# Attention steps of a hybrid decoder layer, reordered: heads first, begun inside the fourth query projection

## What is computed

```python
x = x + 0.5 * SwiGLU_1(rms(x))
u, q, k, v = split(rms(x) @ w_in)         # 512 | 512 | 128 | 128 columns
q, k = rope(rms_head(q)), rope(rms_head(k))
pool = (window_mean_w(u) - u) @ pool_w    # w = 2, 4, 8, 16 for the four groups of 128 channels
attn = softmax with a sink per head, window of 128 keys, 8 heads over 2 key heads
x = x + concat(pool * scale, attn) @ w_out
x = x + 0.5 * SwiGLU_2(rms(x))
```

## Time and profile before

| | us |
|---|---|
| median of 3 runs | 893.75 (893.37 to 893.81) |
| the profiled execution, its own time | 894.7 |
| its span in the trace | 892.6 |
| PE busy in the span | 881.3 |
| DVE busy | 658.9 |
| ACT busy | 393.5 |
| POOL busy | 32.4 |

### The profile page before, as it was taken

One profiled execution on the slowest core, in us unless ns is written; L12 is line 12 of the kernel. 1 busy time (PEld: TensorE's weight loads), 2 busy tenths in 40 slices (PEclk: granted clock), 3 DMA queues, 4 the chain that ended last, 5 costly groups with the idle time before them and its releaser, 6 DMA issues.

```text
span 892.6 us, 17094 instructions
## 1 busy us (share of the span) xinstructions
PE 881.3 (99%) x7118; PEld 864.1 (97%) x7118; DVE 658.9 (74%) x954; ACT 393.5 (44%) x631; POOL 32.4 (4%) x37
## 2 busy tenths in 40 slices
PE   9999999999999999999988999999999999999998
PEld 8999999999999999999867999999999999999998
DVE  7969556997479976743777588997469984699844
ACT  8635213554135544433465446554125552255520
POOL 0000000000000000013322000000000000000000
PEclk9999999999999999999997999999999999999999
DMA  7233313423333323423201313333424424244241
GB/s 270 92 124 126 131 48 122 144 89 95 130 119 119 119 84 121 155 80 106 95 1 62 110 68 118 126 112 102 147 72 154 131 74 153 79 146 130 81 122 60
DMA packets 42892, 98.57 MB, mean 110 GB/s; under 512 B 4128, under 2 KB 4768, under 8 KB 42816
## 3 DMA queue, kind: packets, MB, share of 16 engines
q1 hardware_dynamic: 40912, 94.67, 31.8%
q10 hardware_dynamic: 1904, 2.81, 0.9%
HBM read 93.53 MB, written 3.60 MB: 109 GB/s over the span
## 4 chain that ended last, share of the span: by engine, by line
PE 93%; DVE 4%; ACT 1%; issue 1%; POOLq 0%; POOL 0%; DVEq 0%
PE ps L565 43%; PE ps L693 15%; PE ps L695 15%; PE ps L694 15%; PE ps L596 1%; ACT prob L1315 1%; PE ps L587 1%; DVE small L1799 1%; DVE prob L1815 1%; PE ps L752 1%; PE ps L612 0%; PE ps L966 0%; PE ps L835 0%; DVE wlo L1431 0%; DVE hlo L1558 0%
## 5 line engine op out<-in xcount | busy, mean ns | idle before, releaser
L693 PE MATMUL ps<-xhi,whi 128*128 128x260 f32 (+1 forms) x1092 | 310.2, 284 | 0.1
L695 PE MATMUL ps<-xhi,wlo 128*128 128x260 f32 (+1 forms) x1092 | 310.1, 284 | 0.0
L694 PE MATMUL ps<-xlo,whi 128*128 128x260 f32 (+1 forms) x1092 | 309.7, 284 | 0.0
L693 PEld LDWEIGHTS ps<-xhi,whi 128*128 128x128 f32 x1092 | 205.4, 188 | 0.8 <-issue 0.6
L695 PEld LDWEIGHTS ps<-xhi,wlo 128*128 128x128 f32 x1092 | 205.5, 188 | 0.0
L694 PEld LDWEIGHTS ps<-xlo,whi 128*128 128x128 f32 x1092 | 205.5, 188 | 0.0
L1502 DVE TENSOR_TENSOR wlo<-full,whi 128x1024 fp32r<-128x1024 f32 (+1 forms) x117 | 160.3, 1394 | 0.0
L1049 ACT CAST whi<-raw 128x1024 fp32r<-128x1024 f32 (+1 forms) x76 | 76.3, 1004 | 180.6 <-PE ps L565 171.6
L565 PE MATMUL ps<-hhi,whi 128*128 128x268 f32 (+1 forms) x690 | 140.5, 285 | 0.3
L565 PE MATMUL ps<-hlo,whi 128*128 128x268 f32 (+1 forms) x690 | 140.2, 285 | 0.0
L565 PE MATMUL ps<-hhi,wlo 128*128 128x268 f32 (+1 forms) x690 | 139.8, 284 | 0.0
(11 more groups left out here) (191 smaller groups left out, 1084.8 us busy)
## 6 DMA issues: line engine op xcount, KB each, us to landing
full<-gu SPq DMA_DIRECT2D x78, 512.0 KB, 4.4
raw<-d SPq DMA_DIRECT2D x32, 448.0 KB, 3.4
full<-gu SPq DMA_DIRECT2D x39, 256.0 KB, 2.7
raw<-d SPq DMA_DIRECT2D x16, 512.0 KB, 3.4
raw<-gu SPq DMA_DIRECT2D x10, 512.0 KB, 3.8
raw<-w_in SPq DMA_DIRECT2D x10, 512.0 KB, 3.6
raw<-w_out SPq DMA_DIRECT2D x8, 512.0 KB, 4.5
xT<-x SPq DMA_DIRECT2D x8, 268.0 KB, 5.5
```

The source lines that it names most:

```text
L693: nc.tensor.matmul(dst, whi_t, xhi_t, start=(first and pr == 0), stop=False, skip_group_check=True)
L694: nc.tensor.matmul(dst, whi_t, xlo_t, start=False, stop=False, skip_group_check=True)
L695: last = nc.tensor.matmul(dst, wlo_t, xhi_t, start=False, stop=(pr == KC - 1), skip_group_check=True)
```

## The change

Steps are ordered by head pair first: step i handles block i % 4 and head pair i // 4. Steps 0 to 3 thus need only q0 and q1. The sums of squares, roots and reciprocals of the queries are taken in two halves (q0 and q1, then q2 and q3 with the decode queries). The steps' banks are nsum, turn and pair[1] in turn; all of u0 to u3 and the pool maps use pair[0]; the decode products use the second banks of turn and nsum. PE's, ACT's, DVE's and POOL's lists are written anew. The waits of POOL's window sums for given steps go (after_probs), and so does ACT's wait of the first out_probT for the decode exponential. The buffer prob moves to where upn, p1c, u2c, u4c and t4 lie. Counts of semaphores are adapted.

```diff
-    banks_of = [ps[:, 2:4, :], ps[:, 4:6, :], ps[:, 6:8, :]]
-    outpair = [ps[:, 0:2, :], ps[:, 6:8, :]]
+    banks_of = [nsum, turn, pair[1]]
+    outpair = pair
...
-        return k // 2, 2 * (i % 2) + k % 2
+        return k // 2, 2 * (i // QT) + k % 2
...  PE
-        project(4, half[0])
+        project(4, [0, 1])
         q_sums(0)
-        project(4, half[1])
+        project(4, [2, 3, 4])
+        q_sums(1)
+        project(4, [5, 6, 7])
         project(5, half[0])
-        q_sums(1)
-        project(5, half[1])
-        project(6, half[0])
-        q_sums(2)
-        project(6, half[1])
...
-        project(7, half[0])
-        q_sums(3)
-        project(7, half[1])
-        pool_map(0)
-        scores(0)
-        scores(1)
...
+        scores(0)
+        scores(1)
+        project(5, half[1])
+        project(6, half[0])
+
+        turn_probs(0)
+        scores(2)
+        attend(0)
+        q_sums(2)
+        q_sums(3)
+        project(6, half[1])
+
+        turn_probs(1)
+        scores(3)
+        attend(1)
+        decode_scores()
+        project(7, [0, 1, 2, 3, 4])
+        decode_turn()
+        project(7, [5, 6, 7])
+
+        turn_probs(2)
+        scores(4)
+        pool_map(0)
+        attend(2)
+        project(8, half[0])
+
+        turn_probs(3)
+        scores(5)
+        attend(3)
+        decode_turn_back()
+        project(8, half[1])
+
+        turn_probs(4)
+        scores(6)
+        pool_map(1)
+        attend(4)
+        decode_attend()
+        project(9, half[0])
+
+        turn_probs(5)
+        scores(7)
+        attend(5)
+        project(9, half[1])
+
+        turn_probs(6)
+        pool_map(2)
+        attend(6)
+        turn_probs(7)
+        out_product(1, [0, 1, 4, 5])
+        attend(7)
+        pool_map(3)
+        out_product(1, [2, 6, 7])
+        out_product(0, [0, 1, 4, 5, 2, 6, 7])
+        out_product(0, [3])
+        out_product(1, [3])
         for d in range(2, KD):
...  ACT, behind spread_z(2)
+        q_root(0).then_inc(root_ready, 1)
         split_next(4)
         spread_z(3)
-        split_next(5)
+        exps(0)
         spread_z(4)
+        out_probT(0)
+        exps(1)
+        out_hi(0)
+        q_root(1)
...
+        split_next(5)
+        out_probT(1)
+        exps(2)
+        out_hi(1)
+        split_next(6)
+        exps(3)
...
+        exps(7)
+
+        split_next(9)
+        out_probT(6)
+        pool_hi(2)
+        out_hi(6)
+        out_probT(7)
+        out_hi(7)
+        pool_hi(3)
...  DVE, behind rotate(1)
+        rotate(2)
+        dve.wait_ge(root_ready, 4)
+        half_q = QT * KVH * 2
+        nc.vector.reciprocal(qnrm[:, 1, 0:half_q], qnrm[:, 0, 0:half_q]).then_inc(inv_ready, 1)
         take_z(3)
         split_next(4)
-        rotate(2)
+        dve.wait_ge(inv_ready, 4)
+        maxima(0)
+        rotate(3)
+        maxima(1)
         take_z(4)
-        split_next(5)
-        rotate(3)
+        normalise(0)
+        rotate(4)
+
+        maxima(2)
+        normalise(1)
+        out_lo(0)
...
+        normalise(6)
+        maxima(7)
+        out_lo(5)
+
+        take_u(3)
+        split_next(9)
+        normalise(7)
+        pool_out(2)
+        out_lo(6)
+        out_lo(7)
+        pool_mean(3)
+        pool_out(3)
...  POOL
-        after_probs = {(2, 0): 2, (3, 0): 6, (3, 2): 7}
...
+        window_sums(0)
         window_sums(1)
-        pool.wait_ge(dprob_ready, 1)
         pool_lo(0)
         window_sums(2)
-        pool.wait_ge(prob_ready, 3)
         pool_lo(1)
-        window_sums(3, 0, 2)
-        pool_lo(2)
-        window_sums(3, 2)
         pool.wait_ge(dohi_ready, 1)
...
+        window_sums(3)
+        pool_lo(2)
         pool_lo(3)
```

More of the change, by code:

```diff
@@ L566, in product @@
                                                 start=(k == 0 and w is whi and not lo),
-                                                stop=(k == tiles - 1 and w is wlo))
-            if not ks or ks[-1] == tiles - 1:
+                                                stop=(k == end and w is wlo))
+            if not ks or ks[-1] == end:
                 last.then_inc(unit_done, 1)
@@ L938, in attend, with decode_scores @@
                         last.then_inc(attended, 1)
[L940 to L946, removed]
+        def decode_scores():
+            pe.wait_ge(newk_placed, 1)
+            pe.wait_ge(dq_ready, KVH)
+            pe.wait_ge(probT_ready, 2)
+            for b in range(NDEC):
+                last = nc.tensor.matmul(turn[:, 1, b * HEADS:(b + 1) * HEADS], ckT[:, b, :], dq[:, b, :, :],
@@ L973, in _ @@
-        pool_map(0)
-        scores(0)
-        scores(1)
[L976 to L981, removed]
+            last.then_inc(douts_filled, 1)
         def out_product(d, ks=None):
@@ L988, in out_product @@
                 elif d == 1:
-                    pe.wait_ge(olo_ready, 2 * QT - 2)
+                    pe.wait_ge(olo_ready, 6)
                 else:
                     pe.wait_ge(evacuated, E_OUT + d - 1)
[L993 to L1023, removed]
@@ L1364, in _ @@
         nc.scalar.activation(dsmall[:, 4:5], dsmall[:, 2:3], ACT.Exp).then_inc(dexp_ready, 1)
+        out_hi(2)
+        split_next(7)
+        exps(4)
+        out_probT(3)
         pool_hi(0)
[L1366 to L1384, removed]
+        out_hi(3)
+        exps(5)
+        out_probT(4)
+        split_next(8)
+        out_hi(4)
+        pool_hi(1)
+        exps(6)
+        out_probT(5)
+        act.wait_ge(douts_kept, 1)
+        nc.scalar.copy(mhi[:, NG:NG + GQ, SEQ:NOUT], dout[:, :, :].rearrange("p b j -> p j b")
+                       ).then_inc(dohi_ready, 1)
+        out_hi(5)
+        exps(7)
[6 more added lines that the diff above has]
+        pool_hi(3)
         for d in range(KD):
@@ L1888, in _ @@
         nc.vector.tensor_tensor(dsmall[:, 2:3], dsmall[:, 1:2], dsink, ALU.add).then_inc(dnmax_ready, 1)
-        pool_mean(1)
+        take_u(1)
+        normalise(3)
+        pool_out(0)
+        maxima(4)
+        out_lo(2)
         dve.wait_ge(dexp_ready, 1)
@@ new lines, in _ @@
+        pool_mean(1)
+        split_next(7)
+        normalise(4)
+        maxima(5)
+        out_lo(3)
+        dve.wait_ge(dprobs_filled, 1)
+        nc.vector.tensor_copy(dprobT[:, :], nsum[:, 1, 0:HD]).then_inc(dprobs_kept, 1)
+        take_u(2)
+        normalise(5)
+        pool_out(1)
+        maxima(6)
+        split_next(8)
+        out_lo(4)
+        dve.wait_ge(douts_filled, 1)
+        for g in range(KVH):
+            rows = slice(g * HD, (g + 1) * HD)
+            last = nc.vector.tensor_copy(dout[rows, :, :],
+                                         turn[rows, 1, 0:HD].rearrange("p (b h) -> p b h", b=NDEC)[
+                                             :, :, g * GQ:(g + 1) * GQ])
@@ L1930, in _ @@
+        last.then_inc(douts_kept, 1)
+        pool_mean(2)
+        normalise(6)
[9 more added lines that the diff above has]
+        pool_out(3)
         for d in range(KD):
```

187 lines of the change are left out of this document (77 added, 110 removed).

## The result

The change makes the kernel slower: 898.24 us median of 6 runs (896.42 to 899.89) against 893.78 (893.27 to 895.51), ratio 1.0043, 95% interval 1.003 to 1.0055. A second set of six runs of the same file gave 899.07 beside 893.89, ratio 1.0053 (1.0038 to 1.0068). The ratios and intervals go by all runs of both kernels, so they differ a little from the ratio of the medians: by the medians the loss is 4.5 and 5.2 us, by the ratios 3.8 and 4.7. The forecast was 889.2.

What follows compares the result with a forecast made beforehand. PE, busy 99% of the span, was taken as the bound. 403.5 + 86.8 of work + waits 0.6, 1.2, 2.4, 2.0, 1.95 = 498.5; the walk's 498.15 was taken, 4.5 us under 502.7: median 889.2, range 886.9 to 893.0.

Steps and rivals of the forecast that it cites:

- 4.9 for the clock: PE at 478.0 to 488.7 us: the old order's slow-clock stretch goes, 4.9 of at most 5.1 us taken off.
- I take 479.7: End of normalise(7) on DVE, held beside POOL's sums by 0.6 + 1.0 us; 478.1 if free of them.
- The walk of the lists: All engines' lists followed from scores(0) at 414.0 to output unit 2, which starts at 498.15 against 502.7 before.
- waits of 0.6 and 1.2: PE's two early waits for step probabilities, 0.6 us at about 423 and 1.2 at about 426.
- table loads and SP's late queue: ACT's extra table loads (2 x 1.28 us) and SP's output weights, delayed from 419.5 to 435.7, make PE wait for nothing.
- PE's own work: PE from 403.5 to output unit 2: no stage matmul added or removed, about three fewer switches; 86.8 us of work.
- 0.8 for small gaps in the output units: PE's small idle gaps in the output units, 0.8 us taken off the old trace's 99.2 us.
- free end at 478.1: normalise(7) on DVE ends at 478.1 if POOL's sums do not hold it; 1.6 us less, kept for the range.
- The waits of 2.0 and 1.95: PE waits 2.0 us at pool_map(3) behind pool_mean(3), and 1.95 at output unit 2 for its weight split.
- rival (a): Slow clock returns in the stretch from 474.2 to 480 or 424 to 430; price 3 to 5 us; chance 0.15.
- Rival (b): DVE between 428 and 484, held by 15 untied POOL instructions, becomes a slower bound; up to 896 us; chance 0.11.
- Rival (c): Steps do not begin early: late q1 rotation or half root delays scores(0), up to 3 us, 892; chance 0.07.

Runs made afterwards that it cites:

- a_warm_fit: Changed kernel with empty matmuls, three in front of turn_probs(7) and two in front of pool_map(3), sized to fit those waits; 894.98 us, ratio 1.0014 to the kernel before.
- a_sums_held: Changed kernel with one wait added: POOL's four sums of the last group start only when step 7's probabilities are normalised; 895.71 us, ratio 1.0008 to the kernel before.
- b_warm: Kernel before the change with two empty matmuls of 0.88 us each in its wait in front of attend(5); 892.33 us, ratio 0.9988 to the unedited kernel before.
- a_mean_first: Changed kernel with DVE's pool_mean(3) moved in front of out_lo(6) and out_lo(7); 894.32 us, ratio 1.0000 to the kernel before.
- a_unit0_first: Changed kernel with output unit 0 finished three blocks before output unit 1 instead of one; 896.37 us, ratio 1.0024 to the kernel before.
- b_sums_free: Kernel before the change with POOL's waits for given steps taken out; 897.06 us, ratio 1.0045 to the unedited kernel before.

## Why the prediction was wrong

The step that weighs most is the term "4.9 for the clock": it was booked as a gain, with full clock assumed for the new order, and the new order lost more to the clock than the old one. The second is the end of the lists, "I take 479.7", where the mechanism was right and the size was not. Both are measured at the start of output unit 2, counted from scores(0), as each trace begins a few tenths of a microsecond apart. The forecast had 498.15 - 414.0 = 84.15 us, the changed kernel took 506.61 - 413.82 = 92.8, and a_warm_fit, the same order at full clock, 502.03 - 414.29 = 87.7. So 3.6 of the 8.6 us are there without the clock, and 5.0 are the clock. In a_warm_fit:

```profile
414.29 0.60 PE L922 MATMUL ps<-maskb,identb 128*128 128x512 bf16 x2
...
475.68 1.04 PE L937 MATMUL ps<-fixed,prob 128*128 128x128 f32 x8
...
483.24 1.09 PE L937 MATMUL ps<-fixed,prob 128*128 128x128 f32 x8 [0.61 <-DVE prob L1863]
...
502.03 0.48 PE L571 MATMUL ps<-mhi,whi 128*128 128x260 f32 x2 [1.83 <-DVE wlo L1479]
```

By steps:

- **The walk of the lists** was right in its early half: scores(0) forecast at 414.0 and without a wait, found at 413.8; waits of 0.6 and 1.2 forecast, 0.1 to 0.5 (in four profiles) and 1.04 found; no wait from step 1 to 5, found; table loads and SP's late queue cost nothing, found. The three sets of transfers landed 1.7, 2.1 and 1.5 us behind the end of their issues (the rotations start at 410.56, 418.39 and 427.05), where I took 2.0: right within 0.6 us.
- **PE's own work** was sized 1.2 us short: at full clock turn_probs(6) comes 61.4 us behind scores(0), forecast 60.2. The two sets of sixteen decode products took 1.8 us each where four times the row of 0.34 gives 1.4; the rest is not placed. The sum also takes off 0.8 for small gaps in the output units and puts none back for the new order, which has the same units; the trace of before has only 99.2 - 92.7 - 6.4 = 0.1 us of idle time outside its waits there. The forecast followed the walk, which does not use that term.
- **"I take 479.7"** for normalise(7), the contention at the end, failed in size. turn_probs(7) came at 483.24 in a_warm_fit, 3.25 late counted from scores(0): 1.2 are PE's own work, 1.1 the hold, and 0.9 stand in front of the split, mostly a wait that the sum lacks. The hold: I gave each DVE instruction group one, 0.6 + 1.0 = 1.6. The split was not held at all, and normalise(7) was held three times, 1.03 - 0.16 + 2.93 - 1.14 = 2.7. The wait: the split stood 1.16 us idle for ACT's copy whi, which ACT makes behind exps(7) (the row at 479.87 above; the same 1.16 in a_warm_fit), and a free end at 478.1 leaves only about 0.4 for it. a_sums_held takes the whole hold away: the wait falls by 2.7 and the time by 3.1 us. The wait of 0.9 in front of attend(6), for a copy of ACT that stands behind the same whi, is not in the forecast either; it costs nothing, as turn_probs(7) behind it has 3.4 to wait anyway.
- **The waits of 2.0 and 1.95** at pool_map(3) and unit 2 were right in place and size: 2.3 and 1.8. The forecast waits sum to 8.15 us, against 6.4 in the old order, so on waits alone the change was forecast slower by 1.8. That sign was right in part by luck: at full clock the old order waits 8.0 us (b_warm: 6.1, and 1.9 that its empty matmuls fill), so 8.15 would have been a tie. The changed order waits 10.0 there (a_warm_fit, the filled time counted), 2.0 more.
- **"4.9 for the clock"** turned the forecast to a gain. It was credited in full to the change, as certain, with clock 1.00 assumed after it. Both halves failed. The fall cost the kernel before 3.0 to 3.2 us, not 4.9 (b_warm), as waits reappear when PE is faster. And the changed kernel, forecast with a wait of 2.4, one of 2.0 and one of 1.95 close to one another, fell three times. The rival (a) had this mechanism; it was given 0.15 and one fall, since a stretch with 3.6 us of waits had kept its clock.

Rival (b) named the right engines and the wrong place: in the middle steps the held instructions are covered, and its 15 full microseconds did not come (DVE's scalings are 4.9 us longer in all). Rival (c) did not occur.

At full clock the account closes: before 891.5 (b_warm, six runs), changed 893.7 (a_warm_fit, two runs), 2.3 slower, of which 2.0 are the waits. The clock adds 2.8 to the kernel before (894.3, the median of 72 runs) and 5.0 to the changed one (898.7), 2.2 more. Together 4.4 or 4.5.

## What to carry to other kernels

Do not book a low-clock stretch of the old trace as a gain: ask first what the waits alone give, and then whether the new order has fewer waits near dense work, since the clock followed them here and took the loss from 2.3 to 4.4 us. A reordering that fills the middle moves the waits to the ends, so look at what is left to lay over the last step before the first. And where waits of one engine look useless, find which other engine they keep it away from; price each meeting by how many of the other's instructions lie beside it and which of the two begins first.

## What the runs showed of the hardware

Behind a wait of 1.83 us between dense products stood a low stretch: granted clock 0.55 from 508.2 to 511.5, the fall 1.1 us behind the wait's end. In the kernel before the fall came 0.5 us behind a wait of 1.84 (478.45), but another wait of 1.89 had none. The same list of PE also falls in some profiles and not in others (near 429: yes in the changed kernel and a_mean_first, no in a_sums_held and a_unit0_first), and the mean clock of one kernel varies (0.990 to 0.996 in twelve runs of the changed one). The Trainium skill, TensorE: Matmul & The Clock Gate, Part 1, says that an idle TensorE is throttled and a busy one released. The runs agree in direction, and one fall came inside a wait (483.9); but those at 429.2, 478.45 and 507.8 came with the engine at work again, and in some runs only. That matmuls without a use raise the clock and shorten the time (mean clock 0.9973 against 0.9927, 3.5 us, in a_warm_fit) is shown here directly.

DVE's four scalings take 1.14 us alone, 2.17 beside one POOL instruction, 2.93 in the changed kernel, and 3.52 and 4.10 beside three in b_sums_free: about 0.8 to 1.0 us for each POOL instruction met, nearly POOL's own duration of 1.07. From its chain of waits:

```profile
446.15 3.52 DVE prob L1815 x4
...
479.46 4.10 DVE prob L1815 x4
```

Which of the two is held follows in these traces from which began first. The DVE splits and small two-input instructions that began while a sum ran were held (425.02, 1.87 us, behind a sum of 424.75; 481.01 above); a reciprocal, with one input, was not (445.94 in b_sums_free, 0.18 us inside a sum). A split that began first was not, and the sum was held instead: the split at 479.87 took its 1.23, and the sum at 479.94 took 2.08 where 1.07 is free; the split at 436.72 took 1.21, and the sum at 436.77 took 2.08.

```profile
436.72 1.21 DVE L1473 TENSOR_TENSOR wlo<-raw,whi 128x1024 fp32r<-128x1024 f32 x1
436.77 2.08 POOL L2031 TENSOR_TENSOR wsum<-up 128x528 f32<-128x528 f32 x1 [6.96 <-DVE up L1780]
```

Each held instruction ended 0.02 to 1.1 us behind the one that it met, somewhat less than its own length. The forecast took the hold as a price of the pair of instructions; in these rows it also depends on their order, by less than 0.1 us at 479.87.
